# Forgetting attention: four gate rows of a stacked operand by DMA instead of GpSimd products, and the high parts of queries and keys rounded at two other tiles

## What is computed

```python
k, v, cum_log_f = shared_kv(h, kv_norm, w_kvf, b_f)      # cum_log_f: (heads, 512), running sum of log gates
q = (hn @ wq) * (64 ** -0.5)                             # 16 heads of 64
s = q_t . k_s  + F_t - F_s      for s <= t, else -inf    # F = cum_log_f of the head
p = softmax(s);  o = p @ v;  out = o @ wo
```

## Time and profile before

| | us |
|---|---|
| median of 3 runs | 2156.45 (2152.4 to 2157.42) |
| the profiled execution: its own time | 2157.53 |
| the profiled execution: span | 2155.7 |
| PE busy | 1979.7 (92%) |
| DVE busy | 1110.4 (52%) |
| POOL busy | 1047.3 (49%) |
| ACT busy | 733.4 (34%) |

### The profile page before, as it was taken

The page is one execution under the profiler, slowest core; times in us unless marked ns, Lnnn a source line. Parts: engine busy times, 40 slices in busy tenths (PEclk is TensorE's granted clock), DMA queues, the critical chain, the costliest instruction groups (busy, mean ns, idle before and its releaser), DMA issues.

```text
span 2155.7 us, 30205 instructions
## 1 busy us (share of the span) xinstructions
PE 1979.7 (92%) x9963; PEld 1603.1 (74%) x9963; DVE 1110.4 (52%) x1820; ACT 733.4 (34%) x1233; POOL 1047.3 (49%) x573
## 2 busy tenths in 40 slices
PE   7888998989999999756899999999997799999997
PEld 5677766768887888545778888887876678888886
DVE  6787873654678696689434223132137844132232
ACT  4323234353322322435442222233235643222223
POOL 5465425526765744680454444446444235444442
PEclk9999999999999999889999999999999999999999
DMA  4233002323332333100233333334345413333332
GB/s 142 71 91 100 1 1 64 98 50 88 97 98 85 94 95 90 56 2 0 69 98 98 89 105 90 98 97 99 97 111 124 112 59 97 98 98 92 103 88 88
DMA packets 343417, 179.52 MB, mean 83 GB/s; under 512 B 27951, under 2 KB 335527, under 8 KB 343335
## 3 DMA queue, kind: packets, MB, share of 16 engines
q1 hardware_dynamic: 342592, 177.81, 29.4%
q10 hardware_dynamic: 742, 0.68, 0.1%
HBM read 162.73 MB, written 2.10 MB: 76 GB/s over the span
## 4 chain that ended last, share of the span: by engine, by line
PE 54%; issue 12%; POOL 9%; DVE 9%; POOLq 6%; DVEq 4%; ACT 4%; DMA 2%; SPq 1%; ACTq 0%
PE ACC L1436 15%; PE ACC L1442 15%; PE ACC L1437 15%; POOL WL L1113 7%; POOLq L1123 2%; DVEq L2222 1%; POOLq L1295 1%; POOLq L1283 1%; DVE PTL L2228 1%; ACT WH L550 1%; DMA RAW<-in_w_v_cross_dram 1%; PE ST L1558 1%; PE ST L1560 1%; PE ST L1559 1%; PE O L1558 1%
## 5 line engine op out<-in xcount | busy, mean ns | idle before, releaser
L1113 POOL TENSOR_TENSOR WL<-RAW,WH 128x1024 fp32r<-128x1024 f32 (+1 forms) x308 | 733.4, 2383 | 792.3 <-ACT WH L550 717.7
L1436 PE MATMUL ACC<-PH,WH 128*128 128x512 f32 x1248 | 495.6, 397 | 11.7 <-DVE PL L1962 3.1
L1437 PE MATMUL ACC<-PL,WH 128*128 128x512 f32 x1248 | 489.5, 392 | 0.0
L550 ACT ACTIVATE WH<-RAW 128x1024 fp32r<-128x1024 f32 (+1 forms) x308 | 317.8, 1034 | 490.1 <-PE ACC L1442 414.4
L1436 PE MATMUL ACC<-QH,WH 128*128 128x512 f32 (+1 forms) x1136 | 431.5, 384 | 23.8 <-ACT WH L550 18.1
L1437 PE MATMUL ACC<-QL,WH 128*128 128x512 f32 (+1 forms) x1136 | 426.8, 380 | 0.0
L1442 PE MATMUL ACC<-PH,WL 128*128 128x512 f32 x1248 | 311.1, 391 | 0.0
L1436 PEld LDWEIGHTS ACC<-PH,WH 128*128 128x128 f32 x1248 | 236.5, 190 | 71.1 <-issue 4.7
L1442 PE MATMUL ACC<-QH,WL 128*128 128x512 f32 (+1 forms) x1136 | 272.3, 380 | 9.6 <-POOL WL L1113 9.4
L1437 PEld LDWEIGHTS ACC<-PL,WH 128*128 128x128 f32 x1248 | 236.6, 190 | 49.3 <-issue 1.0
L1442 PEld LDWEIGHTS ACC<-PH,WL 128*128 128x128 f32 x1248 | 234.0, 188 | 52.6 <-issue 3.3
(11 more groups left out here) (416 smaller groups left out, 2436.0 us busy)
## 6 DMA issues: line engine op xcount, KB each, us to landing
RAW<-in_mlp_w_dram SPq DMA_DIRECT2D x128, 512.0 KB, 4.0
RAW<-in_w_gate_dram SPq DMA_DIRECT2D x22, 512.0 KB, 3.7
RAW<-in_w_up_dram SPq DMA_DIRECT2D x22, 512.0 KB, 3.7
RAW<-in_w_in_dram SPq DMA_DIRECT2D x16, 512.0 KB, 3.8
RAW<-in_w_down_dram SPq DMA_DIRECT2D x16, 512.0 KB, 4.0
RAW<-in_ssm_w_glu_dram SPq DMA_DIRECT2D x16, 512.0 KB, 3.8
RAW<-in_w_kvf_dram SPq DMA_DIRECT2D x16, 512.0 KB, 3.9
RAW<-in_w_k_cross_dram SPq DMA_DIRECT2D x8, 512.0 KB, 4.0
```

Of the source, the lines that this page charges most:

```text
L550: act.activation(WH[:, s, 0:kc], RAW[:, s, 0:kc], ACT.Copy).then_inc(w_hi, 1)
L1113: pool.tensor_tensor(WL[:, s, 0:kc], RAW[:, s, 0:kc], WH[:, s, 0:kc], ALU.subtract).then_inc(w_lo, 1)
L1436: pe.matmul(ACC[s][:, 0:n], WH[:, s, k, :], xh[:, k, :], start=(k == 0), stop=False)
L1437: pe.matmul(ACC[s][:, 0:n], WH[:, s, k, :], xl[:, k, :], start=False, stop=False)
```

## The change

The gate rows are no longer computed on POOL. A place of L1 is set to zero once, by a memset on POOL, and then for each pair and each u a DMA copies the four rows of LF into L1. From pair 3 on, when a place is used again, one more DMA for each u first copies four rows of a zero tile over the four rows of the pair before. `stack` now waits for LF (`f_ready`) and for the memset (`zeroed`) ahead of all its DMAs. On ACT the rounding of the queries for pair c + 2 stands at t = 3, that of the keys at t = 5. The waits of PE for `staged` are gone.

```diff
+        ZERO = at("ZERO", [P, T], F32, 184320)
...
+        def landed(c):
+            return 16 * sum(7 + (i > 2) for i in range(c + 1))
...
             def stack(c):
                 b = place(c)
                 sp.wait_ge(split_lo, c + 1)
+                sp.wait_ge(f_ready, 2)
+                sp.wait_ge(zeroed, min(c, 2) + 1)
                 if c >= 2:
                     sp.wait_ge(e_done, TILES["fox"] + 8 * (c - 1) + 4)
                 for u in range(2):
...
                         sp.dma_start(to.bitcast(F32), src.bitcast(F32)).then_inc(stacked[u], 16)
+                    gates, old = 64 * (1 - u) + 2 * c + u, 64 * (1 - u) + 2 * (c - 2) + u
+                    if c > 2:
+                        sp.dma_start(L1[b][old:old + 49:16, u, :].bitcast(F32), ZERO[old:old + 49:16, :]).then_inc(stacked[u], 16)
+                    sp.dma_start(L1[b][gates:gates + 49:16, u, :].bitcast(F32), LF[gates:gates + 49:16, :].bitcast(F32))\
+                      .then_inc(stacked[u], 16)
...
-            def split_high(c):
+            def queries_high(c):
                 if c:
                     for u in range(2):
-                        act.wait_ge(stacked[u], 96 * c)
+                        act.wait_ge(stacked[u], landed(c - 1))
                 act.activation(QHS[:], QT[:, c, :], ACT.Copy).then_inc(split_hi, 1)
+            def keys_high(c):
                 act.activation(KHS[:], KT[:, c, :], ACT.Copy).then_inc(split_hi, 1)
...
-                    if t == 4 and c < 6:
-                        split_high(c + 2)
+                    if t == 3 and c < 6:
+                        queries_high(c + 2)
+                    if t == 5 and c < 6:
+                        keys_high(c + 2)
...
-                elif j == 5:
-                    pool.wait_ge(f_ready, 2)
-                    gates(0)
+                elif j == 3:
+                    pool.memset(L1[2][:].bitcast(F32), 0.0)
+                    pool.memset(ZERO[:], 0.0)
+                    pool.drain().then_inc(zeroed, 1)
                 elif j == 6:
                     split_low(1)
             pool.wait_ge(unit_done, START["wo"])
-            gates(1)
+            for b in (1, 0):
+                pool.memset(L1[b][:].bitcast(F32), 0.0)
+                pool.drain().then_inc(zeroed, 1)
...
             split_low(2)
-            for c in range(2, 8):
-                pool.wait_ge(e_done, TILES["fox"] + 8 * (c - 1) + 4)
-                gates(c)
-                if c < 7:
-                    split_low(c + 1)
+            for c in range(3, 8):
+                split_low(c)
...
-                        pe.wait_ge(stacked[0], 96 * (c + 1))
+                        pe.wait_ge(stacked[0], landed(c))
...
-                    if t % TB == 0:
-                        pe.wait_ge(staged, STAGED[kind] + 2 * c + half + 1)
```

More of the change, by code:

```diff
@@ L360, in build_program @@
             sem(n) for n in ("fw_zero", "fw_in", "fw_hi", "fw_lo", "f_mm", "f_abs", "f_exp", "f_ln", "f_sum", "f_ready"))
-        split_hi, split_lo, stacked, bias_in = (
-            sem("split_hi"), sem("split_lo"), [sem("stacked0"), sem("stacked1")], sem("bias_in"))
+        split_hi, split_lo, stacked, bias_in, zeroed = (
+            sem("split_hi"), sem("split_lo"), [sem("stacked0"), sem("stacked1")], sem("bias_in"), sem("zeroed"))
         y_gain, y_t, y_squared, y_out_of, y_scale, y_dve, y_act, stored = (
@@ L1060, in _, with split_high @@
             act.activation(F[:], F[:], ACT.Ln, bias=ONES[:, 0:1]).then_inc(f_ln, 1)
-            def split_high(c):
+            def queries_high(c):
                 if c:
                     for u in range(2):
-                        act.wait_ge(stacked[u], 96 * c)
+                        act.wait_ge(stacked[u], landed(c - 1))
                 act.activation(QHS[:], QT[:, c, :], ACT.Copy).then_inc(split_hi, 1)
+            def keys_high(c):
                 act.activation(KHS[:], KT[:, c, :], ACT.Copy).then_inc(split_hi, 1)
+            def split_high(c):
+                queries_high(c)
+                keys_high(c)
             def attend_fox():
@@ L1386, in split_low @@
                 pool.drain().then_inc(split_lo, 1)
[L1388 to L1396, removed]
             for j in range(8):
@@ L1568, in scores @@
                     if t == 0:
-                        pe.wait_ge(stacked[0], 96 * (c + 1))
-                        pe.wait_ge(stacked[1], 96 * (c + 1))
+                        pe.wait_ge(stacked[0], landed(c))
+                        pe.wait_ge(stacked[1], landed(c))
                         pe.wait_ge(bias_in, 96 if c else 32)
-                    if t % TB == 0:
-                        pe.wait_ge(staged, STAGED[kind] + 2 * c + half + 1)
                 elif t == 0:
```

## The result

| | before | changed |
|---|---|---|
| median | 2156.87 us (2152.4 to 2157.5, 5 runs) | 2171.26 us (2166.6 to 2174.75, 5 runs) |
| profiled execution: its own time, span | 2157.53, 2155.7 | 2170.25, 2168.5 |
| POOL busy | 1047.3 (49%) | 1032.7 (48%) |

The ratio is 1.0068, with a 95% interval of 1.0053 to 1.0084: the changed kernel is slower, by 14.4 us in the medians (11.4 to 18.1 by the interval). First the page of the changed kernel: engines, the granted clock, the chain that ended last.

The account below looks back on a forecast made before the run. No engine was full; hand-overs between DVE, ACT and PE were taken to bound the stage. 8.5 + 1.7 + 5.8 - 1.4 + 1.6 = 16.2 on 2157.53 gave 2173.7 profiled; median forecast 2172, range 2161 to 2181.

Parts of the forecast that it names:

- Part 1: Front: all of stack(0) waits for f_ready, so the last two wq loads go out later, +8.5 us (8.4 to 9.0).
- Part 2: Wq unit 6: PE's matmuls run at a low clock after the long wait, +1.7 us (0.8 to 3.4).
- Part 3: Group 0: stack(1) waits for its memset and two four-row copies, delaying PE's scores of pair 1, +2.0 us.
- Part 4: QHS to QHS: the stack's landing sets a 15.4 us cycle; +5.8 us by its end, group 0's 2.0 included.
- part 6: SP's queue: occasional slow issues, formerly hidden, count in the cycle, two at 0.8 us: +1.6 us (0 to 2.5).
- Part 5: Group 5: DVE's shorter wait for PTH and faster 128-column division count only there, -1.4 us.
- Only the front: Rival, chance 0.20: the cycle is about as long as the groups anyway; 12.2 us slower, 2168.6 us.
- Dear small copies: Rival, chance 0.15: four-row copies on SP cost 0.64 us each; 5.5 us more, 2177.5 us.
- The clock falls in each group: Rival, chance 0.10: landing waits lower PE's clock in five more groups; 6.5 us more at most, 2178.5 us.
- Not slower: Rival, chance 0.10: relief of DVE and ACT decides, six groups shorten by 8.1 us; 1.5 us slower, 2158 us.

Follow-up runs that it names:

- front alone: Kernel before with the wait for f_ready put ahead of the twelve copies of stack(0), nothing else: 2163.42 us, ratio 1.0038.
- loads first: Changed kernel with the last two wq loads issued ahead of stack(0), nothing else: 2155.54 us, ratio 1.0016 to the kernel before.
- combined kernel: Changed kernel with doubled QHS and KHS, wq loads and four-row copies reordered, smaller memsets, RF semaphores per place, keys at t = 4: 2142.46 us.
- tiles alone: Kernel before with queries rounded at t = 3 and keys at t = 5, POOL's products and twelve copies kept: 2157.79 us, ratio 1.0017.
- old tiles: Changed kernel with queries and keys both rounded at t = 4 again, gate rows still by DMA: 2168.44 us, ratio 1.0059.
- wait moved back: Changed kernel with the twelve copies of stack(0) again ahead of the wait for f_ready, its four-row copies behind: 2164.97 us, ratio 1.0050.

## Why the prediction was right, point by point

The forecast was 2172.0 in a range of 2161 to 2181, the median is 2171.26; the profiled execution was put at 2173.7 and took 2170.25. The sum of 16.2 stands against 17.9 by the ruler, and the 5.1 us upstream are chance. The mechanism held: late loads, a low clock behind the wait, and a landing that ACT waits for in every group. That the time was met to 1 us is in part luck. By stretches the sum had 10.2 for the front, 2.0 for group 0 and 4.0 for the later groups; the ruler has 11.1, 4.4 and 2.3, so an error of 2.4 in group 0 and one of 1.7 behind it point in opposite directions, and the medians lie 3.5 us nearer together than the ruler says. Its steps:

- **Part 1**, +8.5: the loads went out 8.8 later with respect to LF. The price of a four-row copy was mis-sized: 0.40 was taken from a DRAM load on ACT's queue, and it is 0.52 to 0.60, with its gap 0.57 to 0.65. The 64-row copy (0.60, 0.64 with its gap) was the nearer row, though it has 16 times the rows. The rule of the Trainium skill, page "DMA: Bandwidth & Descriptors", section "Why a DMA increments its semaphore by 16 and not by 1", that was weighed there (that the issuing sequencer writes the missing increments itself) fits this price better than the row I preferred; the copies don't show which part of the 0.52 is that. The 0.64 of all twelve was a little high: six 64-row copies take 3.8 us, since the first is issued in 0.50. The delay itself was made and undone on the chip (front alone, loads first).
- **Part 2**, +1.7: 2.3, what the front has beyond the 8.8. The low clock lasted from 1612.6 to 1617.5, 4.9 us and not 3.3.
- **Part 3**, +2.0: PE's first scores of pair 1 stand 2.9 us later behind wq unit 7, and the end of group 0 stands 4.4 us later. One issue of 1.39 us and a gap of 0.3 us lie in stack(1). A term was left out: PE was expected to wait 3 us there and to go on at full clock. It waited 5.03 us, and then ran at a granted clock of 0.50 for 4.6 us. Part 2 had priced just this for the other wait. No run takes the low clock away by itself.
- **Part 4 and part 6**, 15.4 a cycle, +5.8 and +1.6: the exponential of tile 6 in group 5 begins 93.2 us after wq unit 7, against 83.6 before: +9.5 for 7.4. Two of the four cycles were right to 0.2 us (15.33 and 15.22), with the landing 0.4 shorter (1.7 for 2.1, a figure for which the prediction had no row) and the issues 0.3 longer than set. The other two hold a slow issue each: 15.86 one of 1.01 us, 16.43 one of 1.83 us, together 1.7 us more than the usual issue, for the 1.6 of part 6 (of the three slow ones that part 6 counted before, one lies in stack(0) and not in the stage). QHS of pair 2 came 0.7 us later than set, and the first cycle was mis-sized (17.75 for 16.0: KHS came 5.8 us behind QHS, since PE was late and slow). So the miss of 2.1 lies in group 0, and the cycles behind it are right.
- **Part 5**, -1.4: -2.8, from that exponential to the end of the stage. This mark stands right behind the wait of QHS, so part of the 2.8 is only what that wait had delayed; at the PH<-O of pair 5 the loss is 6.5, and 6.7 at the end. Of the two gains that were named, the division's fell: the prediction let KLS hold up a division "as it did before", and it holds the one of tile 7 for 1.54 us in place of 0.97.
- **The rivals.** *Only the front* (parts 1 to 3, 12.2 us) was nearer than it looks: the front and group 0 have 15.5 of the 17.9 us. It fell on the cycle, which does bind, with 19.6 us of waits on ACT; in place of a group of 14.5 us there are 15.2 to 15.3, but two dips of the clock before (the groups of 15.85 and 15.97 us) are one after (16.88). *Dear small copies* was right in its price nearly (0.57 for 0.64) and would have added 3.9 us to the sum; other terms offset it. *The clock falls in each group* fell: the window shows 1.00 over the four cycles from pair 3 to pair 7. *Not slower* fell for the changed kernel; its group of 13.2 us is what the combined kernel has.

What the prediction did not see is what the keys' place does. It took the sixteen copies as the cause of the cycle and the keys' place as one of its terms. The runs show the tiles alone to cost 3.5 us, and the sixteen copies with the old tiles to cost nothing behind group 0. Besides the circle through QHS there is a second one through PTH, which stays when the buffers are doubled, and a division that runs beside KLS.

## What to carry to other kernels

A wait put at the head of a helper holds everything that the queue has behind it: here putting it ahead of twelve copies cost 9.9 us in the front, and issuing the loads ahead of it all gave 11.4 back. Where a single buffer is written again only after its copies have landed, the work from the write to the landing is a circle with a length of its own; add it up (here 15.2 us) and compare it with the pace of the group. When one circle is opened and the pace stays, look for the next one by the distances between equal instructions: a short wait can stand for a long circle. And an edit that moves one instruction moves what runs beside it: look at the durations of the other engines too before the gain is given to one cause. A stage is best cut at marks that the change does not move; here that showed group 0 to hold two thirds of the stage's loss, where the distances between QHS had pointed at the later groups.

## What the runs showed of the hardware

- A copy of four rows of 2 KB within on-chip memory takes SP's queue 0.52 to 0.60 us, a copy of 64 such rows 0.60 in the median, and 15 of the 64 from QHS and KHS in the changed kernel 0.46 to 0.50: the rows hardly count. The next issue starts 0.04 us later.
- From the begin of the last issue to the engine that its landing released: 1.7 us for the four-row copy (1701.79 to 1703.52, and 1705.25 to 1706.99).
- Single issues of 64-row copies took 1.0 to 2.1 us in place of 0.6, two to four times in the stage of each kernel traced. In the circle of the changed kernel they lengthened two cycles from 15.2 or 15.3 to 15.86 and 16.43 us.
- After an idle time of 4.53 us (wait moved back) PE's matmuls started 0.34 and 0.31 us apart, and then 0.43 from 1609.2 to 1612.2, at a granted clock of 0.50; after 10.11 us (changed) they were 0.43 apart from 1613.2 to 1617.5, at 0.50. At full clock they are 0.23 apart. The second stretch is longer than the 3.3 us of the earlier trace rows.
- A DVE division of 512 columns took 0.49 us alone, 1.21 us beside a POOL product of 64 rows (1.03 us), and 1.53 to 1.57 us where it began with a POOL subtraction of 128 rows (1.28 us), in groups 1 to 5 of every kernel with the keys at t = 5. For 128 columns it was 0.71 beside a product and 0.29 alone.
